# Query products ahead of the state products, the query norm inside the ladder of turns, and the transfers into `m1` issued one stage later

## The chip, the cores and the metric

The kernel runs on one core of a Trainium2 chip. Its engines are TensorE (PE, matrix products into PSUM), VectorE (DVE), ScalarE (ACT), GpSimd (POOL) and SyncE (SP), which here only issues transfers. Each engine works through its own list of instructions in order and waits on semaphores for the others. The metric is the time of one execution on the device in microseconds.

## The reference

One block of a network on 512 tokens of width 1024, in fp32. What matters here is the first half:

```python
h = x * (1.0 + sc1) + sh1                       # sc1, sh1 from silu(c) @ w_ada + b_ada
u, cq, ckv, kr = jnp.split(h @ w_in, splits)    # widths 512, 384, 256, 32
y_s5  = _s5_mixer(u, ...)                       # 32 groups of 16 inputs, 64 complex states, a scan over 512 steps
q  = _rmsnorm(cq, q_norm) @ w_uq                # 8 heads x (64 + 32 rotary)
kv = _rmsnorm(ckv, kv_norm) @ w_ukv             # 8 heads x (64 + 64)
y_mla = softmax(mask(q k^T * scale)) v          # causal by chunks of 64
y_mix = concat(_rmsnorm(y_s5), _rmsnorm(y_mla)) @ w_out
```

Behind it come a layer norm and a routed layer of 16384 experts, which take most of the time and are untouched.

## The kernel before

The program is five stages, each a block with a barrier of all engines behind it (`build`): `condition` (modulation, input projection), `project`, `attend`, `mix`, and `query` with `experts`. No engine starts the next stage before every engine has gone through its list. The order inside a stage is written by hand.

The scan is done in 64 chunks of 8 steps. Within a chunk the outputs are a fixed matrix of the inputs, `m1`, whose blocks are copies of `kt32` shifted by one step each: sixteen transfers inside the chip's memory, issued by SyncE (L592 to L595). Between chunks the state is carried by one real scan per part on VectorE (L726), after the states are turned by the powers of a phase, `turn`, which VectorE doubles in six rungs (the ladder, L662 to L672; `TURNS = 6`).

What TensorE does in `project`, in order, with the lines before the change:
- L747 transposes of `xr`, `xi`; L756 sums of squares for the two norms (ScalarE makes `rq`, `rkv` from them, L631, L633); L763 last sums of the modulation, `mod_tail`.
- L775 state products, eight banks `j` = 0 to 7 in PSUM banks 4 to 7. They need `ut` (the inputs, sent to memory and read back in another order, L569 to L574); `j` = 2 waits for `modrow_ready`, since VectorE still reads banks 6 and 7 for `modrow`; `j` of 4 and more wait until VectorE has copied out bank `j`-4 (L712).
- L785 rotary query products, four banks, from `cqn`, the normed query input; they wait until VectorE has copied out banks 5 and up of the state products. VectorE applies the rotation, `rope_q(0)` and `rope_q(1)` (L696 to L700).
- L790 64-wide query products, four banks from `cqn`, copied out by ScalarE (L622).
- L801 products with `bpad`, four banks, each pair behind one `rope_q`; VectorE copies them into `kt32` (L731).
- L809 key and L816 value products from `ckvn`.

VectorE's list: squares; the whole ladder and `mag` (L662 to L674); `rq`'s reciprocal and `cqn` (L677, L679); the same for `rkv`, `ckvn` (L682, L684); `modrow` (L690); the copies L712; `rope_q` twice; turning and scan (L718 to L726); `kt32` (L731); keys' rotation into `kh` (L732 to L736). SyncE's list: `brow`, `u_scr`, `ut`, mask rows into `qh` (L579), `modrow` to memory (L581) when it is ready, mask rows into `kh` (L583), `modc` (L587), and, when `kt32` is complete, the `m1` transfers. In `attend` SyncE clears 26 semaphores and then waits for the landing of the `m1` transfers; `m1` is first read in `mix` (L1139).

Of the kernel before, what the change touches and what calls it, by code (L numbers as in the profile page):

```python
# [12 lines left out]
ALU = mybir.AluOpType  # L13
AXX = mybir.AxisListType.X

P = 128
# [5 lines left out]
S5W, GROUPS, GH, NS = 512, 32, 16, 64  # L22
SK = S5W // P
NQ = GROUPS // 2
CH = 8
# [525 lines left out]
def project(nc, io, k, ps):  # L551
# [10 lines left out]
    @k.block.sync  # L562
    def _(sp):

        b_ada = io["b_ada"]
        for g in range(4):
            sp.dma_start(k.brow[32 * g:32 * g + 32, :, :],
                         bass.AP(b_ada.tensor, b_ada.offset + (4 + g) * 512, [[0, 32], [4 * 512, 2], [1, 512]])).then_inc(k.s_brow, 16)
        sp.dma_start(u_scr.rearrange("(m p) t -> p m t", p=P),  # L569
                     k.uT[:, :, :, :].rearrange("p m s c -> p m (s c)")).then_inc(k.s_uout, 16)  # L570
        sp.wait_ge(k.s_uout, 16)
        for s in range(CH):
            sp.dma_start(k.ut[s * GH:(s + 1) * GH, :, :],
                         u_scr.rearrange("(g h) (s c) -> h g s c", h=GH, s=CH)[:, :, s, :]).then_inc(s_ut, 16)  # L574

        mask = io["mask_rows"]
        for r in range(4):
            for qh in k.qh:
                sp.dma_start(qh[MASK_AT[r], r, :], mask[0]).then_inc(k.s_mask, 16)  # L579
        sp.wait_ge(k.modrow_ready, 1)  # L580
        sp.dma_start(k.mod_scr.rearrange("r g n -> g r n"), k.modrow[0:P:32, :, :]).then_inc(k.s_modrow, 16)  # L581
        for r in range(4):
            sp.dma_start(k.kh[MASK_AT[r], r::4, :],  # L583
                         bass.AP(mask.tensor, mask.offset + ROPE * T, [[T, ROPE], [0, 2], [1, T]])).then_inc(k.s_mask, 16)
        sp.wait_ge(k.s_modrow, 16)
        scr = k.mod_scr
        sp.dma_start(k.modc[:, 3 * DK:5 * DK], bass.AP(scr.tensor, scr.offset + D, [[1, P], [P, 2 * DK]]), allow_slow_non_contiguous=True).then_inc(k.s_modc, 16)  # L587

        sp.wait_ge(k.d2_evac, 16)
        sp.wait_ge(k.m1_zero, 1)  # L590
        m1 = k.m1[:, :, :].rearrange("p (q two) n -> p q two n", two=2)
        for s in range(CH):  # L592
            for g2 in range(2):
                sp.dma_start(m1[s * GH:(s + 1) * GH, :, g2, s * GH:],
                             k.kt32[g2 * GH:(g2 + 1) * GH, :, 0:(CH - s) * GH]).then_inc(k.s_m1, 16)  # L595

    @k.block.gpsimd
    def _(pool):
        nc.gpsimd.memset(k.bpad[:, :, :, :, :], 0.0).then_inc(k.bpad_zero, 1)
# [46 lines left out]
    @k.block.vector  # L646
    def _(dve):
        step = k.dve_steps.on(dve)
        v = nc.vector
        tt = v.tensor_tensor  # L650
        qcol = k.cols[:, ROW_AT["mla_q_norm"]:]
        kcol = k.cols[:, ROW_AT["mla_kv_norm"]:]
        for i in range(QK + KK):
            x = k.cqT[:, i] if i < QK else k.ckvT[:, i - QK]
            tt(k.sq[:, i], x, x, ALU.mult).then_inc(k.sq_ready, 1)

        dve.wait_ge(k.a2_out, 8)
        dve.wait_ge(k.bpad_ready, 1)
        tc, ts = k.turn[:, 0], k.turn[:, 1]
        v.memset(tc[:, :, 0:1], 1.0)  # L660
        step(v.memset(ts[:, :, 0:1], 0.0))
        for i in range(TURNS):  # L662
            n = 1 << i
            c, s = (a[:, i].unsqueeze(2).broadcast_to([P, NQ, n]) for a in (k.turn_c, k.turn_s))
            c0, s0, c1, s1 = tc[:, :, 0:n], ts[:, :, 0:n], tc[:, :, n:2 * n], ts[:, :, n:2 * n]
            t0, t1 = k.sct[:, 0, :, 0:n], k.sct[:, 1, :, 0:n]
            tt(c1, c0, c, ALU.mult)
            tt(t0, s0, s, ALU.mult)
            tt(s1, s0, c, ALU.mult)
            step(tt(t1, c0, s, ALU.mult))  # L670
            tt(c1, c1, t0, ALU.subtract)
            step(tt(s1, s1, t1, ALU.add))  # L672
        v.tensor_copy(k.mag[:, :, 1:], k.mag8[:, :].unsqueeze(2).broadcast_to([P, NQ, NC]))
        step(v.memset(k.mag[:, :, 0:1], 0.0))  # L674

        dve.wait_ge(k.a2_evac, 9)
        step(v.reciprocal(k.rq[:, :], k.rq[:, :]))  # L677
        for i in range(QK):
            ins = v.scalar_tensor_tensor(k.cqn[:, i], k.cqT[:, i], qcol[:, i:i + 1], k.rq[:, :], ALU.mult, ALU.mult)  # L679
        ins.then_inc(k.cqn_ready, 1)  # L680
        dve.wait_ge(k.a2_evac, 10)
        step(v.reciprocal(k.rkv[:, :], k.rkv[:, :]))  # L682
        for i in range(KK):
            ins = v.scalar_tensor_tensor(k.ckvn[:, i], k.ckvT[:, i], kcol[:, i:i + 1], k.rkv[:, :], ALU.mult, ALU.mult)  # L684
        ins.then_inc(k.ckvn_ready, 1)

        dve.wait_ge(k.mod_tail, 1)
        dve.wait_ge(k.s_brow, 64)
        for r in range(2):
            ins = v.scalar_tensor_tensor(k.modrow[:, r], ps[:, 6 + r], k.consts[:, 2 + r:3 + r], k.brow[:, r], ALU.add, ALU.add)  # L690
        step.tell(ins, k.modrow_ready)

        def rope_q(i):
            dve.wait_ge(k.d2_out, 8 + 2 * i + 2)
            q = ps[:, 4 + 2 * i]
            tt(k.ropet[:, :], ps[:, 4 + 2 * i + 1], k.rsin[:, :], ALU.mult)  # L696
            step(tt(q, q, k.rcos[:, :], ALU.mult))
            for r in range(4):
                rows = ROPE_AT[r]
                ins = tt(k.qh[i][rows, r], q[rows], k.ropet[rows, :], ALU.add)  # L700
            step.tell(ins, k.d2_evac, 8 + 2 * i + 2, by=2)

        dve.wait_ge(k.d2_out, 1)
        v.memset(k.ir[:, :, 0:1], 0.0)
        v.memset(k.ii[:, :, 0:1], 0.0)
        for j in range(8):
            part, b = j // 4, j % 4
            dve.wait_ge(k.d2_out, j + 1)
            src = ps[:, 4 + b].rearrange("p (q two c) -> p q two c", two=2, c=NC)
            for g2 in range(2):  # L710
                half = slice(g2 * NS, (g2 + 1) * NS)
                ins = v.tensor_copy((k.ir, k.ii)[part][half, 4 * b:4 * b + 4, 1:], src[half, :, g2, :])  # L712
            ins.then_inc(k.d2_evac, 1)
        dve.wait_ge(k.d2_evac, 8)
        rope_q(0)
        rope_q(1)
        br, bi, t0, t1 = k.ir[:, :, 1:], k.ii[:, :, 1:], k.sct[:, 0, :, 1:], k.sct[:, 1, :, 1:]
        tt(t0, br, ts, ALU.mult)  # L718
        tt(t1, bi, ts, ALU.mult)
        tt(br, br, tc, ALU.mult)  # L720
        step(tt(bi, bi, tc, ALU.mult))
        tt(br, br, t1, ALU.add)
        step(tt(bi, bi, t0, ALU.subtract))
        for part, b in enumerate((k.ir, k.ii)):
            w, m, b = (a.rearrange("p q c -> p (q c)") for a in (k.sct[:, part], k.mag[:, :, :], b[:, :, :]))
            ins = v.tensor_tensor_scan(w, m, b, 0.0, ALU.mult, ALU.add)  # L726
        step(ins)
        dve.wait_ge(k.s_modrow, 16)
        for b in range(4):
            dve.wait_ge(k.d2_out, 12 + b + 1)  # L730
            v.tensor_copy(k.kt32[:, 4 * b:4 * b + 4].rearrange("p q n -> p (q n)"), ps[0:2 * GH, 4 + b]).then_inc(k.d2_evac, 1)  # L731
        tt(k.ropet[:, :], k.krT[:, 1], k.rsin[:, :], ALU.mult)  # L732
        step(tt(k.krT[:, 0], k.krT[:, 0], k.rcos[:, :], ALU.mult))
        for r in range(4):
            rows = ROPE_AT[r]
            tt(k.kh[rows, r::4, :], k.krT[rows, 0].unsqueeze(1).broadcast_to([ROPE, 2, T]),  # L736
               k.ropet[rows, :].unsqueeze(1).broadcast_to([ROPE, 2, T]), ALU.add)

    @k.block.tensor
    def _(pe):  # L740
# [19 lines left out]
        for r in range(2):  # L760
            for g in range(4):
                at = (4 * r + g) * 512
                ins = mm(ps[32 * g:32 * g + 32, 6 + r, :], k.ones[:, 0:32], k.mod_acc[:, at:at + 512], start=True, stop=True,  # L763
                         tile_position=(0, 32 * g))
        ins.then_inc(k.mod_tail, 1)
        pe.wait_ge(k.a2_evac, 8)
        pe.wait_ge(s_ut, 16 * CH)
        for j in range(8):
# [6 lines left out]
                ins = mm(ps[:, 4 + b, (q % 4) * P:(q % 4 + 1) * P], (k.xtr, k.xti)[part][:, q],  # L775
                         k.ut[:, 2 * q:2 * q + 2].rearrange("p a b -> p (a b)"), start=True, stop=True)
            ins.then_inc(k.d2_out, 1)
        pe.wait_ge(k.cqn_ready, 1)
        pe.wait_ge(k.wsw_ready, 1)
        for i in range(2):  # L780
            for sw in range(2):
                pe.wait_ge(k.d2_evac, 5 + 2 * i + sw)
# [1 line left out]
                    w = (k.w_sw if sw else k.w_qr)[:, kt, i].rearrange("p two h c -> p (two h c)")  # L784
                    ins = mm(ps[:, 4 + 2 * i + sw], w, k.cqn[:, kt], start=(kt == 0), stop=(kt == QK - 1))  # L785
                ins.then_inc(k.d2_out, 1)
        for i in range(4):
            pe.wait_ge(k.a2_evac, n - 3)
            for kt in range(QK):
                ins = mm(ps[:, n % 4], k.w_qn[:, kt, 2 * i:2 * i + 2].rearrange("p h c -> p (h c)"), k.cqn[:, kt],  # L790
                         start=(kt == 0), stop=(kt == QK - 1))
            ins.then_inc(k.a2_out, 1)
            n += 1

        pe.wait_ge(k.bpad_ready, 1)
        for b in range(4):
            pe.wait_ge(k.d2_evac, 8 + 2 * (b // 2) + 2)
# [24 lines left out]
def attend(nc, io, k, ps):  # L822
# [122 lines left out]
    @k.block.sync  # L945
    def _(sp):
        for sem in over:
            sp.sem_clear(sem)
        sp.wait_ge(k.s_m1, 16 * 2 * CH)
    for sem in over:  # L950
        nc.release_semaphore(sem)
# [1075 lines left out]
```

## Time and profile before

| | us |
|---|---|
| median of 3 runs (lowest, highest) | 1619.41 (1616.14, 1623.07) |
| the profiled execution, its own time | 1620.23 |
| its span in the trace | 1618.4 |
| TensorE busy | 1525.7 |
| VectorE / GpSimd / ScalarE busy | 1269.3 / 996.8 / 688.2 |
| mean granted clock of TensorE | 0.98 |

Times in the trace count from the span's start. A row of the timeline gives start, duration, engine, line, operation, output and inputs, how many instructions it merges, and in brackets how long the engine had been idle and what ended that. The granted clock is a share of 2.4 GHz; 0.50 is 1.2 GHz.

### The profile page before, as it was taken

Reading aid. Unit: us, or ns where it says so; the run is one execution under the profiler, and the core shown is the slowest. Engines: PE = TensorE matmul, PEld = TensorE weight load, DVE = VectorE, ACT = ScalarE, POOL = GpSimd, SP = SyncE. Lnnn points to the kernel's source line nnn. Section 1 sums busy time; section 2 is a strip of 40 time slices with the busy share of each in tenths; the row PEclk is TensorE's granted clock in tenths of the full one; section 3 lists DMA queues with packets and bytes.
Section 4 is the critical chain, followed back from the end, with each engine's and each line's share of the span. In section 5 each row is a group of like instructions: output and inputs, shape, how many; then the busy total and the mean of one; then the engine's idle time right before and its main releaser. Section 6 shows DMA issues by size and latency. Waiting matters only on the chain.

```text
span 1618.4 us, 21748 instructions
## 1 busy us (share of the span) xinstructions
PE 1525.7 (94%) x7951; PEld 1268.7 (78%) x7951; DVE 1269.3 (78%) x2000; ACT 688.2 (43%) x1273; POOL 996.8 (62%) x608
## 2 busy tenths in 40 slices
PE   6996997978999999999999999999999999999996
PEld 2344575437889999999999998998888888788875
DVE  6768741283889999969887897549989888999997
ACT  2030464204233433358877876344333333333332
POOL 3511000023326777776766887788978888889875
PEclk9997999989999999999999999999999999999998
DMA  9974205412306787778898999999999999999971
GB/s 367 327 216 53 30 1 186 165 52 87 122 27 206 258 277 278 269 266 326 335 361 345 355 376 346 417 333 378 376 379 362 376 376 382 383 370 383 372 267 65
DMA packets 217302, 438.91 MB, mean 271 GB/s; under 512 B 37220, under 2 KB 129892, under 8 KB 215404
## 3 DMA queue, kind: packets, MB, share of 16 engines
q1 hardware_dynamic: 179612, 302.44, 53.2%
q0 software_dynamic: 36864, 134.23, 22.6%
q8 instruction: 63, 1.03, 0.3%
q10 hardware_dynamic: 720, 0.85, 0.2%
q14 instruction: 43, 0.35, 0.1%
HBM read 379.66 MB, written 56.64 MB: 270 GB/s over the span
## 4 chain that ended last, share of the span: by engine, by line
PE 26%; DMA 21%; issue 8%; DVE 8%; ACT 7%; POOL 4%; SPq 2%; POOLq 0%; ACTq 0%; DVEq 0%
DMA u_raw<-in_peer_uT 9%; DMA a_in<-act_scr 7%; DMA v_raw<-in_peer_v 6%; PE ps L1649 5%; PE ps L1650 5%; PE ps L1651 5%; ACT hot1h L1582 3%; POOL vl L1541 3%; DVE ps L1745 2%; PE ps L1327 2%; PE ps L1328 2%; PE ps L1329 2%; DVE w_f L1853 2%; DVE wl L1858 1%; ACT stage L1590 1%
## 5 line engine op out<-in xcount | busy, mean ns | idle before, releaser
L1535 POOL TENSOR_TENSOR utl<-u_raw,uth 128x1024 fp32r<-128x1024 f32 x128 | 307.2, 2401 | 150.3 <-ACT uth L1554 148.9
L1649 PE MATMUL ps<-h2h,uth 128*128 128x384 f32 x1024 | 348.2, 340 | 3.1 <-POOL utl L1535 3.1
L1541 POOL TENSOR_TENSOR vl<-v_raw,vh 128x1024 fp32r<-128x1024 f32 x128 | 311.5, 2435 | 52.4 <-ACT vh L1554 50.4
L1651 PE MATMUL ps<-h2h,utl 128*128 128x384 f32 x1024 | 343.2, 335 | 0.0
L1650 PE MATMUL ps<-h2l,uth 128*128 128x384 f32 x1024 | 342.9, 335 | 0.0
L1672 PE MATMUL ps<-vh,wh 128*128 128x512 f32 x768 | 300.0, 391 | 2.8 <-DVE wl L1858 2.6
L1673 PE MATMUL ps<-vl,wh 128*128 128x512 f32 x768 | 298.9, 389 | 0.0
L1674 PE MATMUL ps<-vh,wl 128*128 128x512 f32 x768 | 298.9, 389 | 0.0
L1853 DVE TENSOR_TENSOR w_f<-a_in,g_in 128x384 f32<-128x384 f32 x128 | 213.0, 1664 | 51.7 <-DMA a_in<-act_scr 50.7
L1554 ACT ACTIVATE vh<-v_raw 128x1024 fp32r<-128x1024 f32 x128 | 135.3, 1057 | 205.9 <-DMA v_raw<-in_peer_v 165.6
L1649 PEld LDWEIGHTS ps<-h2h,uth 128*128 128x128 f32 x1024 | 192.9, 188 | 3.8 <-POOL utl L1535 3.0
L1650 PEld LDWEIGHTS ps<-h2l,uth 128*128 128x128 f32 x1024 | 193.1, 189 | 0.0
L1651 PEld LDWEIGHTS ps<-h2h,utl 128*128 128x128 f32 x1024 | 192.7, 188 | 0.0
L1737 DVE CUSTOM_DVE_ANT_0 junk<-ring,ps 128x1024 bf16<-128x1024 f32 x128 | 150.4, 1216 | 32.6 <-DMA ring<-in_peer_u,row_at 32.3
L1672 PEld LDWEIGHTS ps<-vh,wh 128*128 128x128 f32 x768 | 144.1, 188 | 36.6 <-DVE wl L1858 6.3
L1674 PEld LDWEIGHTS ps<-vh,wl 128*128 128x128 f32 x768 | 144.2, 188 | 29.9
L1673 PEld LDWEIGHTS ps<-vl,wh 128*128 128x128 f32 x768 | 144.2, 188 | 29.6
L1745 DVE SCALAR_TENSOR_TENSOR ps<-ring,w_sp,ps 128x1024 f32<-128x1024 f32 x127 | 162.4, 1279 | 1.7
L1554 ACT ACTIVATE uth<-u_raw 128x1024 fp32r<-128x1024 f32 x128 | 134.9, 1056 | 66.5 <-DMA u_raw<-in_peer_uT 56.9
L1529 POOL DMA_INDIRECT ring<-in_peer_u,row_at x128 | 136.6, 1067 | 23.3 <-issue 12.0
L1529 POOL DMA_INDIRECT ring<-in_peer_v,row_at x128 | 137.1, 1071 | 22.4 <-issue 20.4
L1040 POOL TENSOR_TENSOR x<-x,ln_b 128x1024 f32<-128x1024 f32 x4 | 9.4, 2346 | 198.3 <-DVE x L1115 198.3
(357 smaller groups left out, 2338.5 us busy)
## 6 DMA issues: line engine op xcount, KB each, us to landing
u_raw<-in_peer_uT SPq DMA_DIRECT2D x128, 512.0 KB
v_raw<-in_peer_v SPq DMA_DIRECT2D x128, 512.0 KB
w_ada<-in_w_ada SPq DMA_DIRECT2D x12, 2048.0 KB, 14.6
act_scr<-acts SPq DMA_DIRECT2D x64, 384.0 KB
g_scr<-stage SPq DMA_DIRECT2D x12, 2048.0 KB
g_in<-g_scr SPq DMA_DIRECT2D x32, 768.0 KB
a_in<-act_scr SPq DMA_DIRECT2D x64, 384.0 KB
w_q<-in_peer_w_query SPq DMA_DIRECT2D x8, 1024.0 KB, 5.4
```

The lines of the kernel that those rows point to most:

```text
L1529: nc.gpsimd.indirect_dma_start(k.ring[j % RING][:, :], None, table, bass.IndirectOffsetOnAxis(ap=k.row_at[:, slot:slot + 1], axis=0)).then ...
L1535: tt(k.utl[b % 3][:, :, :].rearrange(f3), k.u_raw[:, b % 4].rearrange(f3), k.uth[b % 3][:, :, :].bitcast(F32).rearrange(f3), ALU.subtract) ...
L1541: tt(k.vl[:, n % 4], k.v_raw[:, n % 4], k.vh[:, n % 4].bitcast(F32), ALU.subtract).then_inc(k.vl_done, 1)
L1554: copy = lambda dst, src: nc.scalar.activation(dst, src, ACT.Copy)
L1649: mm(o, hi, k.h2h[:, kt, SP:T], start=(kt == 0), stop=False)
L1650: mm(o, hi, k.h2l[:, kt, SP:T], start=False, stop=False)
L1651: ins = mm(o, lo, k.h2h[:, kt, SP:T], start=False, stop=(kt == DK - 1))
L1672: mm(o, hi, k.vh[:, n % 4, cols], start=(n == 0), stop=False)
L1673: mm(o, hi, k.vl[:, n % 4, cols], start=False, stop=False)
L1674: return mm(o, lo, k.vh[:, n % 4, cols], start=False, stop=(n == NBLK - 1))
L1745: ins = v.scalar_tensor_tensor(y_sp, row, w, y_sp, ALU.mult, ALU.add)
L1853: tt(k.w_f[:, n % 2].rearrange("p (c t) -> p c t", t=CHK), k.a_in[:, p % 2, n % 2].rearrange("p (c t) -> p c t", t=CHK), k.g_in[:, q % 2, ...
```

## The change

On TensorE the four banks of 64-wide query products move from behind the rotary products to a place ahead of the state products, with the waits for `cqn` and the swapped weights. On VectorE the ladder becomes a function called for rungs 0 to 2, then come `rq`, `cqn`, `modrow`, `rkv`, `ckvn`, then rungs 3 to 5 and `mag`. On SyncE the sixteen `m1` transfers move from the end of `project`, with their two waits, which the barrier makes needless, to `attend`, behind the clearing of the semaphores and ahead of the wait for their landing.

```diff
@@ project, SyncE
-        sp.wait_ge(k.d2_evac, 16)
-        sp.wait_ge(k.m1_zero, 1)
-        m1 = k.m1[:, :, :].rearrange("p (q two) n -> p q two n", two=2)
-        for s in range(CH):
-            for g2 in range(2):
-                sp.dma_start(m1[s * GH:(s + 1) * GH, :, g2, s * GH:],
-                             k.kt32[g2 * GH:(g2 + 1) * GH, :, 0:(CH - s) * GH]).then_inc(k.s_m1, 16)
@@ project, VectorE
-        for i in range(TURNS):
+        def ladder(i):
             n = 1 << i
...
-        v.tensor_copy(k.mag[:, :, 1:], k.mag8[:, :].unsqueeze(2).broadcast_to([P, NQ, NC]))
-        step(v.memset(k.mag[:, :, 0:1], 0.0))
+        for i in range(3):
+            ladder(i)
         dve.wait_ge(k.a2_evac, 9)
         step(v.reciprocal(k.rq[:, :], k.rq[:, :]))
...
         ins.then_inc(k.cqn_ready, 1)
+        dve.wait_ge(k.mod_tail, 1)
+        dve.wait_ge(k.s_brow, 64)
+        for r in range(2):
+            ins = v.scalar_tensor_tensor(k.modrow[:, r], ps[:, 6 + r], k.consts[:, 2 + r:3 + r], k.brow[:, r], ALU.add, ALU.add)
+        step.tell(ins, k.modrow_ready)
         dve.wait_ge(k.a2_evac, 10)
         step(v.reciprocal(k.rkv[:, :], k.rkv[:, :]))
...
         ins.then_inc(k.ckvn_ready, 1)
-        (the modrow lines above stood here)
+        for i in range(3, TURNS):
+            ladder(i)
+        v.tensor_copy(k.mag[:, :, 1:], k.mag8[:, :].unsqueeze(2).broadcast_to([P, NQ, NC]))
+        step(v.memset(k.mag[:, :, 0:1], 0.0))
@@ project, TensorE, behind mod_tail
+        pe.wait_ge(k.cqn_ready, 1)
+        pe.wait_ge(k.wsw_ready, 1)
+        for i in range(4):
+            pe.wait_ge(k.a2_evac, n - 3)
+            for kt in range(QK):
+                ins = mm(ps[:, n % 4], k.w_qn[:, kt, 2 * i:2 * i + 2].rearrange("p h c -> p (h c)"), k.cqn[:, kt],
+                         start=(kt == 0), stop=(kt == QK - 1))
+            ins.then_inc(k.a2_out, 1)
+            n += 1
         pe.wait_ge(k.a2_evac, 8)
         pe.wait_ge(s_ut, 16 * CH)
...
-        pe.wait_ge(k.cqn_ready, 1)
-        pe.wait_ge(k.wsw_ready, 1)
         for i in range(2):
             for sw in range(2):
...
-        (the query products above stood here)
@@ attend, SyncE
         for sem in over:
             sp.sem_clear(sem)
+        (the m1 transfers above, without the two waits)
         sp.wait_ge(k.s_m1, 16 * 2 * CH)
```

## Rows read from the trace of the kernel before

**Rows 1.** The page: busy time, share of the span and instructions of each engine.

```profile
PE 1525.7 (94%) x7951; PEld 1268.7 (78%) x7951; DVE 1269.3 (78%) x2000; ACT 688.2 (43%) x1273; POOL 996.8 (62%) x608
```

**Rows 2.** Timeline of TensorE, projection stage and both ends of the attention stage.

```profile
113.56 1.94 PE L747 MATMUL ps<-ident,xr 128*128 128x128 f32 x16 [0.94 <-PEq L1950]
...
121.47 1.92 PE L763 MATMUL ps<-mod_acc,ones 128*32 128x512 f32 x16
132.60 3.75 PE L775 MATMUL ps<-ut,xtr 128*128 128x128 f32 x16 [9.20 <-DMA ut<-u_scr]
140.91 3.78 PE L775 MATMUL ps<-ut,xtr 128*128 128x128 f32 x16 [4.56 <-DVE modrow L690]
144.48 4.27 PE L775 MATMUL ps<-ut,xti 128*128 128x128 f32 x32
148.59 2.74 PE L785 MATMUL ps<-cqn,w_qr 128*128 128x512 f32 x6
...
158.90 10.46 PE L790 MATMUL ps<-cqn,w_qn 128*128 128x512 f32 x24
169.29 0.41 PE L801 MATMUL ps<-zr,bpad 128*32 128x128 f32 x2
...
176.39 7.13 PE L809 MATMUL ps<-ckvn,w_kn 128*128 128x512 f32 x16
...
191.34 0.91 PE L838 MATMUL ps<-kh,qh 128*128 128x128 f32 x6 [0.94 <-PEq L1950]
...
242.67 1.96 PE L856 MATMUL ps<-v,probT 128*128 128x64 f32 x16
```

**Rows 3.** Timeline of VectorE, projection stage.

```profile
121.01 0.29 DVE L667 TENSOR_TENSOR turn<-turn,turn_c 128x128 f32<-128x128 f32 x1
...
129.35 3.35 DVE L677 RECIPROCAL rq<-rq 128x512 f32<-128x512 f32 x1
...
134.74 3.35 DVE L682 RECIPROCAL rkv<-rkv 128x512 f32<-128x512 f32 x1
...
140.94 0.40 DVE L712 COPY ir<-ps 64x256 f32<-64x256 f32 x1
...
154.02 0.69 DVE L696 TENSOR_TENSOR ropet<-ps,rsin 128x512 f32<-128x512 f32 x1 [4.37 <-PE ps L785]
...
159.17 0.69 DVE L696 TENSOR_TENSOR ropet<-ps,rsin 128x512 f32<-128x512 f32 x1 [1.03 <-PE ps L785]
...
178.67 4.90 DVE L736 TENSOR_TENSOR kh<-krT,ropet 32x1024 f32<-32x1024 f32 x4
```

**Rows 4.** Timeline of GpSimd and ScalarE, projection stage.

```profile
118.53 3.50 POOL L611 MEMSET m<- 128x4096 f32 x1
119.86 0.69 ACT L631 ACTIVATE rq<-ps,eps 128x512 f32<-128x512 f32 x1 [0.31 <-PE ps L756]
...
190.43 0.60 ACT L622 ACTIVATE v<-ps 128x512 f32<-128x512 f32 x1 [1.12 <-PE ps L816]
```

**Rows 5.** Timeline of SyncE's issues, projection stage; last row: landing of `m1`'s transfers.

```profile
126.14 4.29 SPq L579 DMA_DIRECT2D qh<-in_mask_rows  x8
...
177.46 12.24 SPq L594 DMA_DIRECT2D m<-kt  x16
...
DMA to landing us min/median/max: 2.1/4.3/4.9
```

**Rows 6.** Windows: length, busy by engine, granted clock, DMA share, GB/s.

```profile
128.50:129.00 0.50, 0.00 (x0) 0.00 (x0) 0.47 (x2) 0.00 (x0) 0.00 (x0) 0.53 1.46 99
129.00:145.50 16.50, 8.35 (x37) 8.08 (x38) 15.02 (x21) 0.00 (x0) 0.00 (x0) 0.50 0.47 76
...
191.34:200.15 8.81, 7.94 (x35) 6.67 (x36) 5.51 (x11) 5.70 (x23) 0.00 (x0) 0.62 0.01 2
...
193.50:200.00 6.50, 6.50 (x27) 5.50 (x26) 3.87 (x8) 3.55 (x18) 0.00 (x0) 0.50 0.00 0
...
200.25:244.60 44.35, 41.96 (x271) 32.64 (x269) 19.12 (x34) 26.73 (x76) 0.00 (x0) 1.00 0.00 1
```

More of the change, by code:

```diff
@@ L685, in _ @@
         ins.then_inc(k.ckvn_ready, 1)
[L687 to L691, printed above, removed]
+        for i in range(3, TURNS):
+            ladder(i)
+        v.tensor_copy(k.mag[:, :, 1:], k.mag8[:, :].unsqueeze(2).broadcast_to([P, NQ, NC]))
+        step(v.memset(k.mag[:, :, 0:1], 0.0))
         def rope_q(i):
@@ L786, in _ @@
                 ins.then_inc(k.d2_out, 1)
[L787 to L793, printed above, removed]
         pe.wait_ge(k.bpad_ready, 1)
@@ L948, in _ @@
             sp.sem_clear(sem)
+        m1 = k.m1[:, :, :].rearrange("p (q two) n -> p q two n", two=2)
+        for s in range(CH):
+            for g2 in range(2):
+                sp.dma_start(m1[s * GH:(s + 1) * GH, :, g2, s * GH:],
+                             k.kt32[g2 * GH:(g2 + 1) * GH, :, 0:(CH - s) * GH]).then_inc(k.s_m1, 16)
         sp.wait_ge(k.s_m1, 16 * 2 * CH)
```

## The prediction

> **What bounds the kernel now.** I read the first page, then the timelines of the projection stage engine by engine, then the granted clock by windows. The page gives TensorE busy 1525.7 us, 94% of the span [rows 1]; the chain of waits that it prints begins only at 367 us and says nothing of the stretch that is edited, so the timelines must do. The kernel is five stages with a barrier between each pair, so a stage ends when its slowest engine ends, and everything behind it moves by what that engine gains.
>
> The projection stage runs from 113.56 to 191.34 us on TensorE [rows 2]. In it TensorE stands still twice: 9.20 us until the transfers of `ut` have landed, 4.56 us until VectorE has written `modrow`. From 140.91 it works without a stop: state products (L775) to 148.59, rotary query products (L785) to 158.90, the 64-wide query products (L790) to 169.29, `bpad` products (L801) to 176.39, key and value products to 190.4; ScalarE copies out the last of them until 191.03 [rows 4], and the barrier adds 0.31. VectorE's own list ends at 178.67+4.90 = 183.57 [rows 3], and SyncE issues the last of the sixteen `m1` transfers at 177.46+12.24 = 189.70 [rows 5]. So three ends lie in a row: TensorE/ScalarE 191.03, SyncE 189.70, VectorE 183.57. A gain on the first alone is worth 1.3 us before SyncE would set the end.
>
> **The change, part by part.** I rebuild the stage on the new order.
>
> *Query norm between the ladder's steps.* VectorE ends the third rung where rung four begins now, 121.01 [rows 3]. ScalarE has written `rq` at 119.86+0.69 = 120.55 [rows 4], so there is no wait. Reciprocal and three products take from 129.35 to 134.74, where the next reciprocal starts, 5.39 us [rows 3]. They end at 121.01+5.39 = 126.40. `modrow` follows at once (L763 ended at 123.39, the rows of `b_ada` landed long before), then `rkv`, `ckvn`, rungs four to six, `mag`. VectorE does the same instructions as before and stood idle for none of them before, so it reaches the copies of the state products (L712) at 140.94 again. No gain, no loss there.
>
> *Query products first.* TensorE is free at 121.47+1.92 = 123.39, waits for `cqn` until 126.45, 3.1 us. The weights are no wait: GpSimd has swapped them before it clears `m1` at 118.53 [rows 4]. The four banks take 169.29-158.90 = 10.39 us [rows 2] and end at 126.45+10.3 = 136.8. The 9.20 and the 4.56 us of standing are thereby filled: `ut` lands by 132.6, `modrow` is ready near 128. ScalarE copies the banks out as they come; it has nothing else to do there.
>
> *State products.* The first four banks have no wait on VectorE now. Sixteen records take 140.91 to 144.48 at the lower clock (0.50), 0.223 us each; at the upper 0.112 [rows 2, 6]. So banks one to four take 3.57 us at 2.4 GHz: 136.8 to 140.3. Bank five needs VectorE to have copied bank one: 140.94 and two copies of 0.43, 141.85 [rows 3]. Banks five to eight: another 3.57, to 145.45. VectorE copies a bank in 0.88 us and TensorE fills one in 0.89, so neither falls behind. The rotary products, which began at 148.59, begin at 145.45: **3.14 us earlier**.
>
> *From the rotary products to the end.* VectorE's first rope begins 5.43 us after L785 begins, the second 10.58 us after (154.02 and 159.17 against 148.59) [rows 2, 3], and from the second rope to the end of its list are 183.57-159.17 = 24.40 us with no wait. New: 145.45+10.58 = 156.03, end 180.43. TensorE goes straight from L785 (ends 155.76) to `bpad`: two banks to 159.3, a wait for the second rope (156.03+4.12 = 160.15), two banks to 163.7, then key and value products, 190.4-176.39 = 14.0, to 177.7; ScalarE 0.6 later, 178.3. So VectorE sets the end now, at 180.43 instead of ScalarE's 191.03: **10.60 us**, and TensorE has 2.1 us to spare.
>
> *The `m1` transfers.* Left in place, they would start after the fourth copy of `kt32`, 177.46-3.14 = 174.32, and their issue would end 12.24 us later, at 186.56: the reordering alone would give 191.03-186.56 = 4.47. Moving them removes SyncE from the stage's end. In the attention stage SyncE has nothing else: issue from about 182 (behind the clearing of 26 semaphores, which it did before too) to 195, landing at most 4.9 us later [rows 5], 200. The attention stage then has some 37 us to run (its last products now end at 242.67+1.96 = 244.63, less 10.6 is 234) [rows 2], and nothing in it reads `m1`. The cover is wide: the transfers would have to take 37 us longer to cost anything. What is queued behind them on SyncE is the wait for their landing and the barrier, no load. Against the attention's own speed I price their traffic at nothing, since the earlier transfers moved beside key and value products that kept their pace; the bound above is an estimate of 2% of the attention's 53.3 us, 1 us.
>
> *The clock.* TensorE's granted clock fell at 128.5 to 129.0, some 5 us into the first standstill, and stayed at 1.2 GHz until 145.5 [rows 6]; it was low again from 193.5 to 200.0, after short gaps only [rows 6]. So the new 3.1 us gap before the query products, and the new gap of about 2.9 us (177.8 to 180.7) before the attention stage, may each bring a fall. The price at the first, from the length of the second low stretch, some 6.8 us with its edges: at half speed it puts the query products' end 3.4 us later, of which 1.5 us are the cover (TensorE waits from 140.3 to 141.85 anyway): 1.9 at most. A fall half as long costs 0.2. I take 0.2. At the attention stage a low stretch lies in the first 9 us already (mean clock 0.62) [rows 6]; one that starts 2 us sooner meets the smallest score tiles and costs between nothing and 2 us. I take nothing.
>
> The Trainium skill, "TensorE: Matmul & The Clock Gate", section "Why this matters for your kernels", warns against idle gaps between bursts of matmuls, since the engine comes back from them at the lower clock. That speaks against an order which opens gaps ahead of two stretches that had none. The trace agrees that gaps bring falls, but the old order had both longer gaps and 16.5 us at the lower clock in the same place, so by the rule too the query and state products come out no worse than computed with the 1.9 us.
>
> **Sum.** 10.60 less 0.2 is 10.4 us. The profiled execution took 1620.2 us (span 1618.4); it becomes 1609.8. The median of the three runs is 1619.41, 0.8 below it: **1609.0 us**.
>
> **The rivals.**
>
> *A. Only the reordering's part is paid.* If something other than SyncE's issues holds the stage, for example `modrow`'s or the mask rows' transfers late on SyncE, the end goes back toward 186.6. For it: SyncE's list is serial. Against it: the masks' issues end at 126.14+4.29 = 130.43 and the key masks need 1.8 us after that [rows 5]. Time 1619.4-4.5 = 1614.9.
>
> *B. The clock takes part of it back.* Both gaps bring long falls: 1.9 and 2 us, and the attention keeps the 1 us of contention. Gain 10.6-4.9 = 5.7, time 1613.7; with one of them 1611 to 1612.
>
> *C. Slower.* One mechanism: the attention stage, entered from a gap and with small tiles, stays at the lower clock instead of rising after 9 us. TensorE was busy 41.96 of the 44.35 us that it ran at the upper clock there [rows 6]; at half speed nearly every one of these is paid twice. From 10.6 us more at the lower clock on the gain is gone, and all of them would give 1619.4-10.6+42 = 1651. Against it: at the lower clock TensorE was busy 6.50 of 6.50 us and rose from that.
>
> *D. Two or three us more.* The low stretches in the attention and the mix stage fall on cheaper places. 1606 to 1608.
>
> **How the numbers follow.** Forecast (sum right within 2.3 us, D included) 0.74; B 0.17; A 0.06; C 0.03. A difference of 0.5%, 8.1 us, is about what a measurement of this kernel can tell from no change, so the line lies at 1619.4-8.1 = 1611.3, 2.3 us above my forecast. The forecast's case and a little of B lie below it: faster 0.75. Same takes the rest of B and A, 0.22; slower is C, 0.03. The three runs of before spread from 1616.1 to 1623.1, 3.5 us to either side, which a median halves. Range 1605.0 to 1614.5: D's gain below, B in full above; A and C are left out.
>
> **What would show it.** Right: query products from 126.4, no wait for `ut` or `modrow`, L712 from 140.9, L785 near 145.5, VectorE's last `kh` at 180.4, the first score product near 180.8, `m1` issued behind it. Wrong: L785 later than 147 (a fall of the clock), a stage end that follows TensorE or SyncE rather than VectorE, an attention stage longer than 53.3 us by over 2 us, or a wait in the mix stage longer by what the projection gained.

## The result and the profile after

| | before | changed |
|---|---|---|
| median of 7 runs (lowest, highest), us | 1620.81 (1616.14, 1628.61) | 1611.67 (1607.38, 1613.52) |
| ratio of the two, 95% interval | | 0.9937 (0.9915 to 0.9960) |
| span of the profiled execution, us | 1618.4 | 1610.7 |

0.9937 is 10.2 us less on 1620.8; 1619.41 times 0.9937, the time to set beside the forecast of 1609.0, is 1609.2. The same kernel was timed again on another occasion: 0.9936 (0.9913 to 0.9959), median 1609.95 of 6 runs.

The timeline of TensorE in the projection stage of the changed kernel, with the first product of the attention stage; these rows answer to [rows 2]:

```profile
113.06 1.94 PE L744 MATMUL ps<-ident,xr 128*128 128x128 f32 x16 [0.94 <-PEq L1951]
...
120.97 1.92 PE L760 MATMUL ps<-mod_acc,ones 128*32 128x512 f32 x16
126.02 10.57 PE L768 MATMUL ps<-cqn,w_qn 128*128 128x512 f32 x24 [3.12 <-DVE cqn L673]
136.42 3.73 PE L781 MATMUL ps<-ut,xtr 128*128 128x128 f32 x32
141.30 3.84 PE L781 MATMUL ps<-ut,xti 128*128 128x128 f32 x32 [1.15 <-DVE ir L709]
144.98 2.74 PE L789 MATMUL ps<-cqn,w_qr 128*128 128x512 f32 x6
...
163.34 7.13 PE L805 MATMUL ps<-ckvn,w_kn 128*128 128x512 f32 x16
170.31 7.03 PE L812 MATMUL ps<-w_v,ckvn 128*128 128x512 f32 x16
180.26 0.91 PE L834 MATMUL ps<-kh,qh 128*128 128x128 f32 x6 [2.92 <-PEq L1951]
```

The waits for `ut` and `modrow` are gone; 3.12 us ahead of the query products and 1.15 us ahead of bank five have taken their place. The barrier now keeps TensorE waiting 2.92 us, not 0.94: it is no longer among the last.

VectorE (answers to [rows 3]), then ScalarE's last copy and SyncE, three timelines of the same kernel:

```profile
120.50 3.35 DVE L671 RECIPROCAL rq<-rq 128x512 f32<-128x512 f32 x1
123.89 2.08 DVE L673 SCALAR_TENSOR_TENSOR cqn<-cqT,cols,rq 128x512 f32<-128x512 f32 x3
...
140.41 0.40 DVE L709 COPY ir<-ps 64x256 f32<-64x256 f32 x1
...
150.40 0.69 DVE L693 TENSOR_TENSOR ropet<-ps,rsin 128x512 f32<-128x512 f32 x1 [2.93 <-PE ps L789]
...
155.55 0.69 DVE L693 TENSOR_TENSOR ropet<-ps,rsin 128x512 f32<-128x512 f32 x1 [1.03 <-PE ps L789]
...
175.05 4.91 DVE L733 TENSOR_TENSOR kh<-krT,ropet 32x1024 f32<-32x1024 f32 x4
```

```profile
177.38 0.60 ACT L614 ACTIVATE v<-ps 128x512 f32<-128x512 f32 x1 [1.12 <-PE ps L812]
```

```profile
130.81 0.67 SPq L581 DMA_DIRECT2D mod_scr<-modrow  x1
...
182.30 12.31 SPq L948 DMA_DIRECT2D m<-kt  x16
```

VectorE ends at 175.05+4.91 = 179.96, ScalarE at 177.98, and the first score product starts 0.30 us behind VectorE. SyncE has issued nothing for 44 us by then; its sixteen transfers come in the attention stage.

All stages of all profiled executions, in us. A stage is counted on TensorE, from its first instruction to that of the next stage (projection: first transpose to first score product; attention: to the first product with `spad`; mix: to the first transpose of the keys; rest: to the end of the span).

| kernel | projection | attention | mix | rest |
|---|---|---|---|---|
| before | 77.78 | 56.56 | 119.85 | 1250.65 |
| changed | 67.20 | 55.35 | 118.38 | 1256.71 |
| changed, again | 67.20 | 56.54 | 120.04 | 1251.16 |
| order only | 73.47 | 56.52 | 120.20 | 1250.31 |
| transfers only | 77.15 | 56.54 | 120.07 | 1250.28 |
| norm behind the ladder | 77.12 | 56.54 | 120.12 | 1249.44 |
| products in the old place | 74.70 | 54.80 | 119.80 | 1254.04 |
| keys on GpSimd | 70.31 | 55.60 | 118.96 | 1253.29 |
| keys on GpSimd, rung in the gap | 70.29 | 58.17 | 119.52 | 1254.38 |
| keys in the gap | 65.99 | 56.57 | 120.05 | 1250.92 |
| keys on GpSimd later (two executions) | 65.50, 65.50 | 58.18, 56.16 | 119.68, 118.80 | 1248.15, 1251.35 |
| the same, rung behind the ropes | 65.99 | 56.57 | 119.89 | 1247.27 |

The projection stage is 10.58 us shorter, in both profiles of the changed kernel to the hundredth. (All other stages in the table but those of "keys on GpSimd later" rest on one execution each.) The first pair of profiles differs by 7.7 us only, as the rest of the changed one was 6.06 us longer, less 0.50, 1.21 and 1.47 us that start, attention and mix were shorter. That rest scatters between 1247.3 and 1256.7 over the thirteen executions, whose code is the same from there on. So the cause is read from the stage, and the worth of it from the many timed runs.

### The profile page after: what moved, and what is told of

The parts are those of the page before. It is cut to its first block, busy times and chain, and to the rows that moved or that the text cites. A ratio compares the mean times of both kernels' runs of the same rounds, so it can differ in the third digit from the quotient of the medians.

```text
span 1610.7 us, 21748 instructions
## 1 busy us (share of the span) xinstructions
PE 1522.4 (95%) x7951; PEld 1264.9 (79%) x7951; DVE 1264.9 (79%) x2000; ACT 687.4 (43%) x1273; POOL 991.9 (62%) x608
## 4 chain that ended last, share of the span: by engine, by line
PE 40%; DMA 16%; POOL 6%; ACT 6%; issue 4%; DVE 4%; SPq 1%; POOLq 0%; ACTq 0%; DVEq 0%
DMA u_raw<-in_peer_uT 8%; PE ps L1650 7%; PE ps L1651 7%; PE ps L1652 7%; DMA v_raw<-in_peer_v 5%; DMA a_in<-act_scr 4%; PE ps L1673 4%; POOL vl L1542 4%; PE ps L1674 4%; PE ps L1675 4%; ACT hot1h L1583 3%; PE ps L1328 2%; POOL ring L1530 2%; PE ps L1329 2%; PE ps L1330 2%
## 5 line engine op out<-in xcount | busy, mean ns | idle before, releaser
L1854 DVE TENSOR_TENSOR w_f<-a_in,g_in 128x384 f32<-128x384 f32 x128 | 208.6, 1631 | 51.9 <-DMA a_in<-act_scr 51.0
L1530 POOL DMA_INDIRECT ring<-in_peer_u,row_at x128 | 132.4, 1034 | 23.4 <-issue 12.2
L1567 ACT ACTIVATE acts<-ps 128x384 f32<-128x384 f32 x128 | 62.5, 488 | 165.5 <-PE ps L1652 165.2
## 6 DMA issues: line engine op xcount, KB each, us to landing
g_scr<-stage SPq DMA_DIRECT2D x12, 2048.0 KB, 10.2
```

The lines of the kernel that those rows point to most:

```text
L1530: nc.gpsimd.indirect_dma_start(k.ring[j % RING][:, :], None, table, bass.IndirectOffsetOnAxis(ap=k.row_at[:, slot:slot + 1], axis=0)).then ...
L1854: tt(k.w_f[:, n % 2].rearrange("p (c t) -> p c t", t=CHK), k.a_in[:, p % 2, n % 2].rearrange("p (c t) -> p c t", t=CHK), k.g_in[:, q % 2, ...
```

## The experiments

The first four take the change apart: two lists (TensorE, VectorE), each in old or new order, and the transfers in either stage.

**Order only.** The new orders, with the sixteen transfers back in `project`:

```diff
@@ project, SyncE, behind modc
+        sp.wait_ge(k.d2_evac, 16)
+        sp.wait_ge(k.m1_zero, 1)
+        (the sixteen transfers)
@@ attend, SyncE
-        (the sixteen transfers)
         sp.wait_ge(k.s_m1, 16 * 2 * CH)
```

> The new order on TensorE and VectorE, with the sixteen transfers into m1 left at the end of the projection stage. Stage length is counted from the first transpose to the first score product: 77.8 us before, 67.2 after. Theory (a stage ends with the latest of its lists): SyncE starts its sixteen issues when VectorE has made the last copy of kt32, 60.75 us into the stage, needs 12.3 us, and the barrier 0.3: 73.4 us, 4.4 shorter than before, total about 1616. Rival (the issues overlap with what follows and do not hold the stage): 67 us, as in the changed kernel.

Measured: stage 73.47 us, 4.31 shorter than before; ratio 0.9983 (0.9959 to 1.0007). SyncE's timeline, and TensorE's with the clock in two windows:

```profile
174.56 11.72 SPq L594 DMA_DIRECT2D m<-kt  x16
```

```profile
126.45 12.26 PE L776 MATMUL ps<-cqn,w_qn 128*128 128x512 f32 x24 [3.12 <-DVE cqn L681]
...
145.70 2.74 PE L797 MATMUL ps<-cqn,w_qr 128*128 128x512 f32 x6
...
186.97 1.62 PE L842 MATMUL ps<-kh,qh 128*128 128x128 f32 x6 [8.91 <-PEq L1954]
```

```profile
127.50:130.50 3.00, 3.00 (x5) 1.35 (x4) 2.97 (x2) 0.00 (x0) 0.00 (x0) 0.50 1.43 93
130.75:146.00 15.25, 15.25 (x84) 10.76 (x83) 14.69 (x37) 4.73 (x8) 0.07 (x1) 1.00 0.58 80
```

SyncE's issues end at 186.28, TensorE stands 8.91 us at the barrier for them. Of the 10.58 us, 6.3 hang on the moved transfers. The execution also shows a fall of TensorE's clock that the changed kernel's two profiles lack: same gap of 3.12 us, then 3 us at 0.50, query products 12.26 us instead of 10.57. The rotary products start 32.20 us into the stage instead of 31.92: of 1.69 us the wait ahead of bank five has swallowed all but 0.28.

**Transfers only.** The kernel before with the SyncE part of the change:

```diff
@@ project, SyncE
-        sp.wait_ge(k.d2_evac, 16)
-        sp.wait_ge(k.m1_zero, 1)
-        (the sixteen transfers)
@@ attend, SyncE
+        (the sixteen transfers)
         sp.wait_ge(k.s_m1, 16 * 2 * CH)
```

> The old order on TensorE and VectorE, with the sixteen transfers moved to the attention stage. Theory: SyncE's list ended 1.3 us ahead of ScalarE's, so its removal changes nothing, stage 77.8 us within 0.3, total as before. Rival (issues or traffic beside the key and value products slow them or the barrier): stage 75 to 76.5 us. Second rival (transfers in the attention stage slow it): attention longer than 56.6 us by 1 to 2.

Measured: 77.15 us, ratio 1.0003 (0.9983 to 1.0023). The 0.63 us below before, more than the 0.3 that I allowed, are as much as the rotary products start sooner (34.41 us into the stage against 35.03), where the clock was back at 1.00 for part of the state products, so they lie ahead of the transfers and are not theirs. Attention 56.54 against 56.56. Alone the transfers' move is worth nothing.

**Norm behind the ladder.** The changed kernel with VectorE's old order:

```diff
-        for i in range(3):
+        for i in range(TURNS):
             ladder(i)
+        (mag; rq, cqn; rkv, ckvn; modrow, in the order of before)
-        (rq, cqn; modrow; rkv, ckvn; rungs 3 to 5; mag)
```

> The changed kernel, but VectorE runs the whole ladder, then the query norm, the key norm and modrow, as before; TensorE keeps the query products in front. Theory: cqn is ready 21.2 us into the stage, TensorE idles 11 us and its clock falls, the query products take 10.4 us and 2 to 3 more at the lower clock, the rotary products start about 41 us into the stage instead of 31.9, and VectorE ends the stage 35.3 us later: 75 to 77 us, only 1 to 3 shorter than before. Rival (the order on TensorE alone carries the gain): 67 to 69 us.

Measured: 77.12 us, 0.1 above the range that I gave; ratio 1.0016 (0.9981 to 1.0050). TensorE's timeline:

```profile
136.97 13.56 PE L767 MATMUL ps<-cqn,w_qn 128*128 128x512 f32 x24 [11.46 <-DVE cqn L675]
150.37 3.73 PE L780 MATMUL ps<-ut,xtr 128*128 128x128 f32 x32
```

The query products wait 11.46 us for `cqn` and cost 3.0 us more than at the upper clock. With the old norm their new place is worth 0.03 us against the run before this one.

**Products in the old place.** The changed kernel with TensorE's old order:

```diff
-        (waits for cqn and wsw, four banks of w_qn products, ahead of the state products)
...
+        (the waits ahead of the rotary products, the four banks behind them)
```

> The changed kernel, but the four banks of 64-wide query products go back behind the rotary products; VectorE keeps its new order and the m1 transfers stay in the attention stage. Theory: the wait for modrow is gone, the state products start at 19.1 us into the stage at the lower clock, the rotary products at 31.8 to 33, VectorE would end at 67 to 68, but TensorE still has 10.4 us of query products in its line and ends last, through ScalarE: stage 74.5 to 76 us, 2 to 3 shorter than before. Rival (the earlier modrow carries the gain): 67 to 68 us.

Measured: 74.70 us, inside the computed range. TensorE's timeline:

```profile
134.13 5.44 PE L772 MATMUL ps<-ut,xtr 128*128 128x128 f32 x32 [10.64 <-DMA ut<-u_scr]
...
155.92 10.46 PE L787 MATMUL ps<-cqn,w_qn 128*128 128x512 f32 x24
...
188.36 0.91 PE L835 MATMUL ps<-kh,qh 128*128 128x128 f32 x6 [0.94 <-PEq L1952]
```

The wait for `ut` is back, the query products stand late again, and the barrier's 0.94 us show TensorE with ScalarE as the last to end. The ratio is 1.0012 (0.9992 to 1.0033): the 3.1 us that the stage gained are not seen in the total, whose interval leaves out a gain of that size.

With the transfers out of the way, the four corners are 77.15 (both old), 77.12 (TensorE new), 74.70 (VectorE new) and 67.20 (both new). TensorE's new order alone gives 0.03 us, VectorE's 2.45; together 9.95.

**The changed kernel again**, to see whether the 6 us of the first profile's last stages belong to the change:

> The changed kernel once more, on the chip of the next two. Theory: the projection stage is 67.2 us from first transpose to first score product, at most 2 us more if TensorE's clock falls in the 3.1 us gap ahead of the query products; the experts' stage behind is not lengthened by the change, it only scatters by some us from execution to execution, so the ratio to the kernel before stays near 0.9935. Rival (the 6 us by which the stages behind the first query product were longer in the one profiled execution belong to the change): ratio 0.996 to 0.998, and again about 1251 us behind the first query product.

Measured: 0.9936 (0.9913 to 0.9959), stage 67.20, rest 1251.16. The rival asked for a long rest again (its 1251 us are counted from the first query product, which is 1256 in this table's count) and a ratio of 0.996 or more. Neither came, so it falls.

**Keys on GpSimd.** Is it VectorE that sets the end now? Its last 6.2 us are taken away:

```diff
@@ GpSimd, behind the clearing of m1
+        gtt(k.krT[:, 1], k.krT[:, 1], k.rsin[:, :], ALU.mult)
+        step(gtt(k.krT[:, 0], k.krT[:, 0], k.rcos[:, :], ALU.mult))
+        (wait for mod_tail, then the four sums into kh, each behind the last)
@@ VectorE, end of project
-        (the two products and the four sums)
```

> The changed kernel with the rotation of the keys (two products and four sums, 6.2 us at the end of VectorE's list) moved to GpSimd, behind its clearing of m1. Theory (VectorE sets the end, TensorE with ScalarE 2.2 us ahead of it): the stage ends with ScalarE's last copy, 65.2 us, 2.0 shorter, and no more. Rival (GpSimd's six instructions slow VectorE's ladder and norms beside them): stage 66.5 to 69 us. If TensorE and not VectorE set the end: 67.2, unchanged.

**The same, rung in the gap.** Rungs 3 and 4 stay, `ladder(5)` and `mag` go between the copies L712 and `rope_q(0)`:

> As the one before, and the last rung of the ladder with mag (4.7 us) moved on VectorE from ahead of the copies of the state products to behind them, where VectorE waits 2.9 us for the first rotary product. Theory: VectorE reaches the copies before TensorE has filled a bank, the 1.15 us wait ahead of bank five is gone, the rotary products start at 30.5 us into the stage instead of 31.9, ScalarE ends the stage: 63.7 us, 3.5 shorter than the changed kernel, total 1607 to 1608. Rival (the rung pushes the first rope back by more than TensorE gains): 65 us or more.

Measured: 70.31 and 70.29 us, both 3.1 longer than the changed kernel; ratios 0.9948 (0.9932 to 0.9964) and 0.9966 (0.9948 to 0.9984). My theory missed by 5 and 6.6 us. The rival of the first, that GpSimd slows VectorE, names the right mechanism, but its 66.5 to 69 us were still too little. Timeline of the first kernel, both engines:

```profile
122.47 3.35 DVE L680 RECIPROCAL rq<-rq 128x512 f32<-128x512 f32 x1
123.48 1.28 POOL L606 TENSOR_TENSOR krT<-krT,rsin 128x512 f32<-128x512 f32 x1
124.72 1.26 POOL L607 TENSOR_TENSOR krT<-krT,rcos 128x512 f32<-128x512 f32 x1
125.86 6.24 DVE L682 SCALAR_TENSOR_TENSOR cqn<-cqT,cols,rq 128x512 f32<-128x512 f32 x3
126.06 8.25 POOL L611 TENSOR_TENSOR kh<-krT 32x1024 f32<-32x1024 f32 x3
132.03 1.40 DVE L687 SCALAR_TENSOR_TENSOR modrow<-ps,consts,brow 128x512 f32<-128x512 f32 x2
133.46 3.35 DVE L690 RECIPROCAL rkv<-rkv 128x512 f32<-128x512 f32 x1
```

The three `cqn` products take 6.24 us instead of 2.08 beside GpSimd's sums; the reciprocals (one input) and `modrow` (one of two inputs in PSUM) keep their 3.35 and 1.40. TensorE waits 4.2 us longer for `cqn`, and in that longer gap its clock falls: it is at 0.50 from about 130 to 137 us, and the query products take 12.91 us, 2.3 more. Less 1.4 us for the shorter wait ahead of bank five and 2.0 because VectorE's shortened list no longer sets the end, that is the 3.1 us.

The Trainium skill, "SBUF — State Buffer", section "Who interferes with whom", has the rule: an exclusive lock on a port pair shared by VectorE and GpSimd. VectorE wants it when both its inputs lie in SBUF and GpSimd reads SBUF at the same time, or when it runs in a two-port mode. The trace agrees: the products with two SBUF inputs are the ones that wait, and GpSimd's sums beside them read SBUF.

**Keys on GpSimd later.** The same six instructions behind a wait for four banks of state products, so that they lie beside VectorE's copies out of PSUM and its ropes:

```diff
         gtt = nc.gpsimd.tensor_tensor
+        pool.wait_ge(k.d2_out, 4)
```

> The key rotation on GpSimd as in the run in which the cqn products took 2.8 us each in place of 0.75, but started when four banks of state products are done, so that it lies beside VectorE's copies out of PSUM, its wait and its ropes, none of which reads two tensors in SBUF. Theory (an instruction of VectorE with two inputs in SBUF waits out the GpSimd instruction in flight, others don't): cqn products back at 0.75 us, copies at 0.43, rotary products at 31.9, stage 65.2 us. Rival (any VectorE instruction beside GpSimd's sums is slowed): copies above 0.5 us each, stage 67 us or more.

> The key rotation on GpSimd beside the copies of the state products, once more and timed. Theory: stage 65.2 us, or 65.5 where TensorE's clock falls in the gap ahead of the query products (1.7 us of lower clock, of which 1.4 are covered by the wait ahead of bank five); ratio to the kernel before near 0.992. If the 65.5 of the first look was chance: 67.

Measured: 65.50 us both times, both with the fall of the clock; ratio 0.9929 (0.9904 to 0.9955). The three `cqn` products, of a group's own statistics (minimum, median, maximum in ns), in the kernel above and in this one:

```profile
L682 DVE SCALAR_TENSOR_TENSOR cqn<-cqT,cols,rq x3: 752/2821/2827, 125.9 to 129.3; 128x512 f32<-128x512 f32 x3
```

```profile
L682 DVE SCALAR_TENSOR_TENSOR cqn<-cqT,cols,rq x3: 744/744/750, 126.5 to 127.8; 128x512 f32<-128x512 f32 x3
```

In the first, one product ran in 0.75 us before GpSimd's sums began, and two took 2.8 us each. The copies of the state products have the same median, 422 ns, in both kernels, though GpSimd's work lies beside them in the second only. With the interference avoided, taking 6.2 us from VectorE brings 1.7 us, not 6.2: VectorE had set the end, and ScalarE had ended only 2.0 us before it.

**Keys in the gap.** Without GpSimd: `mag`, the two key products and one sum in VectorE's wait ahead of the first rope:

```diff
         dve.wait_ge(k.d2_evac, 8)
+        (mag; the two products on krT; the first of the four sums)
         rope_q(0)
```

> The changed kernel with mag, the two key products and the first of the four key sums moved, on VectorE itself, into its wait of 2.9 us ahead of the first rope (3.3 us of work); GpSimd gets nothing. Theory (no fault of GpSimd's can come in, VectorE sets the end of the changed kernel by 2.2 us): VectorE reaches the copies of the state products 0.7 us sooner, the rotary products start at 31.2 us into the stage, VectorE ends 2.5 us sooner on top, ScalarE's last copy ends the stage: 64.5 us, 2.7 shorter than the changed kernel, ratio to the kernel before about 0.992. Rival (the first rope is pushed back and takes the bpad products with it): 66 to 68 us.

Measured: 65.99 us, ratio 0.9929 (0.9904 to 0.9955). That is 1.5 us more than computed, for two reasons. VectorE's and GpSimd's timelines show the first:

```profile
146.97 2.79 DVE L710 COPY mag<-mag 128x1024 f32<-128x1024 f32 x1
...
152.38 0.69 DVE L691 TENSOR_TENSOR ropet<-ps,rsin 128x512 f32<-128x512 f32 x1
```

```profile
145.70 3.51 POOL L605 MEMSET spad<- 128x4096 f32 x1 [23.96 <-PE ps L786]
```

The copy of `mag`, 0.69 us in the changed kernel, ended only after GpSimd's clearing of `spad` had (149.21 us). This fits the lock's other case, a fast copy: 1024 elements in 0.69 us, where a product of that size takes 1.23 (L715 in the changed kernel). No run varies the copy alone. The first rope was pushed back, the `bpad` products waited 0.71 us for it, and 0.5 us of that reached the stage's end through ScalarE, which is the rival's mechanism. The other 1.0 us is the clock: it fell in the gap (query products 12.26 us), which put the rotary products at 32.20 instead of 31.2.

**Rung behind the ropes.** Keys on GpSimd later, and `ladder(5)` with `mag` behind `rope_q(1)`:

```diff
-        for i in range(3, TURNS):
+        for i in range(3, 5):
             ladder(i)
-        (mag)
...
         rope_q(1)
+        ladder(5)
+        (mag)
```

> The same, and on VectorE the last rung of the ladder with mag behind the second rope instead of ahead of the copies. Theory: TensorE no longer waits ahead of bank five, the rotary products start at 30.5 us into the stage, VectorE's list becomes nearly as long as ScalarE's again (64.0 against 63.5): stage 64.3 us without a fall of the clock in the gap. With a fall the cover is gone and its 1.7 us are paid in full: rotary products at 32.2, stage 66.0. Rival (a fall costs 0.3 whatever the order): 64.6.

Measured: the clock fell (12.26 us again), rotary products at 32.21, stage 65.99; ratio 0.9931 (0.9907 to 0.9955). The fall's 1.7 us are paid in full here, by the computed start of 30.5 us without one (the one profile of this kernel has the fall): the wait that covered it is removed. The three versions at 65.5 to 66.0 us beat the changed kernel in the stage by 1.2 to 1.7 us; in the total their ratios of 0.993 cannot be told from its 0.9937.

## Why the prediction was right

Forecast: 10.4 us less, 1609.0; measured 10.2 less by the ratio, 1609.2. That the totals agree to 0.2 us is luck: the ratio's interval runs from 6.5 to 13.8 us less. By it, my line of 1611.3 is not cleared with certainty either, as its upper end is 1612.9. What carries the judgement is the stage, forecast 10.6 us shorter without a fall of the clock and measured 10.58 without one. The steps, counted from the first transpose of the stage:

| | forecast | changed | 
|---|---|---|
| query products start | 12.89 | 12.96 |
| state products start | 23.24 | 23.36 |
| VectorE at the copies | 27.38 | 27.35 |
| rotary products start | 31.89 | 31.92 |
| ScalarE's last copy ends | 64.74 | 64.92 |
| VectorE's list ends | 66.87 | 66.90 |
| first score product | 67.18 | 67.20 |

*Query products first, norm between the rungs.* Right within 0.12 us. The corners say what the forecast's sum left unsaid: the two are one edit. Each alone leaves TensorE either without `cqn` or without a product to fill the gap with.

*The end goes to VectorE.* Right, and tested by taking its last 6.2 us away: 1.7 us came, the 2.0 us to ScalarE's end less the 0.28 of a fall of the clock.

*The transfers.* The forecast gave 4.47 us to the reordering without their move; 4.31 measured. Alone, the move brought nothing. Cover in the attention stage: issued from 182.30 to 194.61, in flight at most 5.0 us, landed by 199.6, 36 us before the mix stage, the first that reads `m1`. I bounded their traffic's cost at 1 us; none is seen. The attention stage of the transfers alone was as long as before (56.54 and 56.56 us). TensorE's timeline from the third score product of the second query block to the first of the third block, six heads, before and changed:

```profile
201.85 0.65 PE L838 MATMUL ps<-kh,qh 128*128 128x256 f32 x2
...
210.68 0.86 PE L838 MATMUL ps<-kh,qh 128*128 128x384 f32 x2
```

```profile
189.57 0.65 PE L834 MATMUL ps<-kh,qh 128*128 128x256 f32 x2
...
198.40 0.86 PE L834 MATMUL ps<-kh,qh 128*128 128x384 f32 x2
```

8.83 us in both, both at the upper clock (granted 1.00), and with the transfers in flight for most of the second only (DMA share 0.42, against 0.00 before).

*The clock.* I took 0.2 us for a fall ahead of the query products. Seven profiles have that gap of 3.1 us at the same place; the clock fell in five (0.28 us each where the wait ahead of bank five was still there), not in the two of the changed kernel. In the attention stage I took nothing; windows over the whole stage, of the changed kernel, of the products in the old place and of the keys on GpSimd later:

```profile
180.26:235.61 55.35, 48.58 (x304) 38.23 (x305) 25.29 (x46) 35.36 (x102) 0.00 (x0) 0.97 0.16 23
```

```profile
188.36:243.16 54.80, 47.64 (x304) 36.92 (x305) 25.22 (x46) 35.32 (x102) 0.00 (x0) 1.00 0.16 23
```

```profile
181.19:239.37 58.18, 52.78 (x305) 41.75 (x305) 25.37 (x46) 35.45 (x102) 0.00 (x0) 0.88 0.16 22
```

The same work takes 54.80 us with no low stretch and 58.18 with one of 13.5 us, 1.6 more than before. So the price that rival B put on it (2 us) was of the right size. The term was left at nothing with reason: before had such a stretch too, and the changed kernel's two profiles gave -1.21 and -0.02 us. The gap of 2.9 us ahead of the stage, which I feared, shows no effect: the three executions with it took 55.35, 56.54 and 56.54 us, the eight with a gap of 0.94 between 54.80 and 58.18, the two longest among them.

*The rivals.* A had its 4.47 us right, but nothing else of SyncE's held the stage. C did not happen: the clock rose every time. D came in one profile of the changed kernel, 1.21 us in the attention and 1.47 in the mix stage (TensorE busy 97.58 us there, not 99.07, at the same mean clock of 0.91), and not in the other (0.02 less and 0.19 more). What stays open is the total of the products in the old place, whose interval leaves out the 3.1 us that its stage gained; its rest was 1254.04 us, in the upper part of the scatter, and no run here tells why.

## What to carry to other kernels

Where stages are closed by a barrier, write down when each engine's list ends: the gain of an edit stops at the next list, and an edit worth nothing alone (the transfers) can carry over half of the gain of another. Two moves that hand one value on, the norm on one engine and its products on the other, should be priced together. A list that waits elsewhere is a cover for falls of the clock; removing the wait removes the cover. Before work goes to GpSimd, look at what VectorE does beside it: here products with two inputs in SBUF waited behind GpSimd instructions that read SBUF, and a fast copy behind a memset.

## What the runs showed of the hardware that I had not expected

- Two of VectorE's three `cqn` products, 0.75 us each otherwise, took 2.8 us each beside GpSimd sums of 2.3 to 2.7 us; a copy of 1024 fp32 elements from SBUF to SBUF took 2.79 us instead of 0.69 beside a GpSimd memset, while the ladder's small products, which have two inputs in SBUF too, kept 0.2 us beside another memset (L603 in the changed kernel).
- GpSimd's sums over 32 partitions and 1024 elements took 2.34 us each in the kernel with the keys on GpSimd later, nearly as long as its differences over 128 partitions and 1024 elements (L1535 on the page of the kernel before, 2401 ns).
- The same gap of 3.1 us in TensorE's work brought a fall of the clock in five executions and none in two.
